# All 16 tiles of x loaded at once at the start of the projection, in place of two buffers in turn

## The reference

```
p = x @ w_in                       # (tokens, 2560) -> q | k | v | glu_a | glu_b
u = glu_a * sigmoid(glu_b)         # conv path: depthwise, width 31, LayerNorm, swish
o = differential attention(q, k, v)        # prompt: causal; sample: over the paged cache
x = LayerNorm(alpha * x + concat(o, conv) @ w_o)
x = LayerNorm(alpha * x + MoE(x))          # 64 experts, top 8, one shared expert
```

## Time and profile before

| what | us |
|---|---|
| median of 3 runs | 4477.3 |
| lowest, highest | 4462.62, 4480.28 |
| the profiled execution | 4473.9 |
| its span | 4472.2 |

### The profile page before, as it was taken

The page is one execution under the profiler, slowest core; times in us unless marked ns, Lnnn a source line. Parts: engine busy times, 40 slices in busy tenths (PEclk is TensorE's granted clock), DMA queues, the critical chain, the costliest instruction groups (busy, mean ns, idle before and its releaser), DMA issues. The chain is left out here.

```text
span 4472.2 us, 68787 instructions
## 1 busy us (share of the span) xinstructions
PE 3796.6 (85%) x20727; PEld 2500.4 (56%) x20729; DVE 2218.8 (50%) x4207; ACT 1589.5 (36%) x3240; POOL 1237.1 (28%) x1067
## 2 busy tenths in 40 slices
PE   6999995888698898858882879999999999999970
PEld 3444443666566665634441656667666676677640
DVE  1700994777565554435556224544444443434438
ACT  1011212666554444424341224443334433433420
POOL 0102211000033333300000754444444444444430
PEclk7999997999899999988885999999999999999985
DMA  3003327340199999931113329997888977877956
GB/s 104 16 19 135 140 92 150 68 87 20 56 386 396 386 403 386 386 135 62 61 61 105 103 82 270 272 266 180 228 229 217 269 185 163 227 177 187 263 130 213
DMA packets 358934, 817.65 MB, mean 183 GB/s; under 512 B 31720, under 2 KB 211304, under 8 KB 320358
## 3 DMA queue, kind: packets, MB, share of 16 engines
q0 software_dynamic: 125600, 512.88, 38.4%
q1 hardware_dynamic: 233166, 302.54, 21.1%
HBM read 659.59 MB, written 156.10 MB: 182 GB/s over the span
## 5 line engine op out<-in xcount | busy, mean ns | idle before, releaser
L1586 POOL DMA_INDIRECT y_s<-y_rows,scatter_now x322 | 539.7, 1676 | 417.6 <-DVE scatter_now L1755 244.5
L1645 PE MATMUL y_ps<-down_w,hiddenT 128*128 (+1 forms) x1416 | 640.3, 595 | 1.4 <-DVE y_rows L1756 1.4
L201 PE MATMUL p_bank<-xT,wcol 128*128 128x512 f32 (+1 forms) x1600 | 600.1, 535 | 5.0 <-DMA wcol<-in_w_in_dram 3.3
L1654 PE MATMUL gate_up_ps<-gu_high,x_highT 128*128 128x512 f32 x1416 | 573.5, 405 | 35.1 <-DVE x_lowT L1737 23.8
L1656 PE MATMUL gate_up_ps<-gu_high,x_lowT 128*128 128x512 f32 x1416 | 557.2, 393 | 0.0
L1655 PE MATMUL gate_up_ps<-gu_low,x_highT 128*128 128x512 f32 x1416 | 555.4, 392 | 0.0
L201 PEld LDWEIGHTS p_bank<-xT,wcol 128*128 128x128 f32 x1600 | 281.2, 193 | 306.5 <-issue 304.7
L1645 PEld LDWEIGHTS y_ps<-down_w,hiddenT 128*128 128x128 f32 x1416 | 255.7, 191 | 258.7 <-issue 258.2
L1743 DVE TENSOR_TENSOR gu_low<-gu_raw,gu_high 128x1024 fp32r<-128x1024 f32 x260 | 301.1, 1221 | 111.4 <-ACT gu_high L1693 106.8
L1578 POOL DMA_INDIRECT x_rows<-x_s,gather_now x179 | 179.8, 1005 | 591.5 <-DVE gather_now L1731 522.0
L1765 DVE TENSOR_TENSOR hidden<-silu_gate,gate_up_ps 128x256 f32<-128x256 f32 x177 | 74.2, 419 | 520.9 <-ACT silu_gate L1715 520.9
(11 more groups left out here) (264 smaller groups left out, 5485.7 us busy)
## 6 DMA issues: line engine op xcount, KB each, us to landing
gu_raw<-in_w_gate_dram SPq DMA_DIRECT2D x64, 1024.0 KB, 12.0
gu_raw<-in_w_up_dram SPq DMA_DIRECT2D x64, 1024.0 KB, 15.6
down_w<-in_w_down_dram SPq DMA_DIRECT2D x64, 1024.0 KB, 6.6
wcol<-in_w_in_dram SPq DMA_DIRECT2D x20, 512.0 KB, 3.9
x_s<-x SPq DMA_DIRECT2D x17, 512.0 KB, 2.6
xin<-in_x_prompt_dram SPq DMA_DIRECT2D x16, 512.0 KB, 3.6
out_dram<-rows POOLq DMA_DIRECT2D x8, 1024.0 KB, 7.7
k_high<-k_high_s POOLq DMA_DIRECT2D x16, 512.0 KB, 23.9
```

The lines of the kernel that those rows point to most:

```text
L201: mm = nc.tensor.matmul(bank[c][:, 0:n], wcol[u][:, k, :], xT[:, k, s:s + n], start=(k == 0), stop=(k == KT - 1))
L1586: pool.indirect_dma_start(out=g.y[half], out_offset=bass.IndirectOffsetOnAxis(ap=to[half][:], axis=0), in_=y[half][:], in_offset=None, com ...
L1645: mm = nc.tensor.matmul(y_ps[half][:], hT[:, k, :], down[:, w(half, k)], start=(k == 0), stop=(k == F // P - 1))
L1654: nc.tensor.matmul(out, x_high[:, k, :], both(gu_high, k), start=(k == 0), stop=False)
```

## The change

The 16 tiles of x get 16 places in SBUF: the two `xin` buffers, and for the other 14 halves of the prompt's part of the four units, of the gate, of `conv_sum` and of `rows1`, all of which the projection writes later. SyncE issues the 16 loads one behind the other with no wait. They count on four semaphores, one for tiles 0 and 1, one for 2 to 5, one for 6 to 10, one for 11 to 15; TensorE waits for the whole of a tile's group. The memset of `xin0` moves to behind VectorE's copy of tile 1; the sample's load is issued behind it, behind all 16, and counts on the first group's semaphore (48 in all). The loops over pairs on TensorE, ScalarE and VectorE become straight code over 17 tiles.

```diff
+        room = [xin[0][:], xin[1][:]] + [t[:, at + half * D:at + (half + 1) * D] for t, at in
+                                         [(glu, PAST) for glu in units] + [(gate, 0), (conv, 0)] for half in range(2)]
+        room += [rows[1][:].rearrange("p t f -> p (t f)")[:, half * D:(half + 1) * D] for half in range(2)]
...
-        x_in, w_arrived = (x_in0, x_in1), (w_in0, w_in1)
+        w_arrived = (w_in0, w_in1)
+        x_in = sems(nc, ctx, *[f"x_in{t}" for t in range(4)])
+        GROUP, PART = [0, 2, 6, 11, QT], [0] * 2 + [1] * 4 + [2] * 5 + [3] * 5
...
-            def load_x(i):
-                for u in range(2):
-
-                    wait(sp, xt_ready, (2 * i + u - 1) * 2)
-                    sp.dma_start(xin[u][:], g.x_prompt[ds(i * 2 * P + u * P, P), :]).then_inc(x_in[u], 16)
-            loop(sp, QT // 2, load_x)
+            for t in range(QT):
+                sp.dma_start(room[t], g.x_prompt[t * P:(t + 1) * P, :]).then_inc(x_in[PART[t]], 16)
             sp.wait_ge(x_zeroed, 1)
             sp.dma_start(xin[0][0:TAIL, :], g.x_sample).then_inc(x_in[0], 16)
 
-            sp.wait_ge(x_in[0], 16 * (QT // 2 + 1))
+            sp.wait_ge(x_in[0], 48)
             sp.dma_start(g.x_tail, xin[0][:]).then_inc(tail_out, 16)
...
-            def turn_x(u, tile, loaded):
-                pe.wait_ge(x_in[u], loaded)
+            def turn_x(u, tile):
+                n = PART[tile] if tile < QT else 0
+                pe.wait_ge(x_in[n], 16 * (GROUP[n + 1] - GROUP[n]) if tile < QT else 48)
+                x = room[tile if tile < QT else 0]
                 for half, copied in ((0, xt_act), (1, xt_dve)):
 
                     wait(pe, copied, tile - 1)
                     for k in range(4):
                         mm = nc.tensor.transpose(bank[2 * u + half][:, k * P:(k + 1) * P],
-                                                 xin[u][:, (4 * half + k) * P:(4 * half + k + 1) * P], g.ident[:])
+                                                 x[:, (4 * half + k) * P:(4 * half + k + 1) * P], g.ident[:])
                     mm.then_inc(xt_ready, 1)
-
-            def turn_pair(i):
-                for u in range(2):
-                    turn_x(u, 2 * i + u, 16 * i + 16)
-            loop(pe, QT // 2, turn_pair)
-            turn_x(0, QT, 16 * (QT // 2 + 1))
+            for tile in range(TT):
+                turn_x(tile % 2, tile)
...
-            loop(dve, QT // 2, keep_pair)
-
-            dve.wait_ge(xt_ready, 2 * (QT - 1))
-            nc.vector.memset(xin[0][:], 0.0).then_inc(x_zeroed, 1)
-            keep_x(0, QT, SEQ)
+            for tile in range(TT):
+                keep_x(tile % 2, tile, tile * P)
+                if tile == 1:
+                    nc.vector.memset(xin[0][:], 0.0).then_inc(x_zeroed, 1)
```

More of the change, by code:

```diff
@@ L119, in in_projection @@
         bank = [ctx.enter_context(nc.psum_tensor(f"p1_bank{b}", [P, 512], F32)) for b in range(8)]
-        (small_in, state_turned, state_kept, zeroed, x_in0, x_in1, x_zeroed, xt_ready, xt_act, xt_dve, w_in0, w_in1,
+        (small_in, state_turned, state_kept, zeroed, x_zeroed, xt_ready, xt_act, xt_dve, w_in0, w_in1,
          acc_ready, feat_ready, glu_ready, last_turned, last_kept, last_out, conv_step, conv_out, stored0,
          stored1, rows_ps, rows_ready, rows_out0, rows_out1, tail_out, high_ready, low_ready, parts_out) = sems(
-            nc, ctx, "small_in", "state_turned", "state_kept", "units_zeroed", "x_in0", "x_in1", "x_zeroed",
+            nc, ctx, "small_in", "state_turned", "state_kept", "units_zeroed", "x_zeroed",
             "xt_ready", "xt_act", "xt_dve", "w_in0", "w_in1", "acc_ready", "feat_ready", "glu_ready", "last_turned",
@@ L332, in keep_x @@
                                       bank[2 * u + 1][:].rearrange("p (k t) -> p k t", k=4)).then_inc(xt_dve, 1)
-            def keep_pair(i):
-                for u in range(2):
-                    keep_x(u, 2 * i + u, i * (2 * P) + u * P)
-            loop(dve, QT // 2, keep_pair)
-            dve.wait_ge(xt_ready, 2 * (QT - 1))
-            nc.vector.memset(xin[0][:], 0.0).then_inc(x_zeroed, 1)
-            keep_x(0, QT, SEQ)
+            for tile in range(TT):
+                keep_x(tile % 2, tile, tile * P)
+                if tile == 1:
+                    nc.vector.memset(xin[0][:], 0.0).then_inc(x_zeroed, 1)
             dve.wait_ge(zeroed, H + 1)
```

## The result

The changed kernel takes 4431.5 us (median of 5 runs, 4428.4 to 4433.1) against 4476.2 us before (5 runs, 4462.6 to 4480.3). The ratio is 0.9915, with a 95% interval of 0.9903 to 0.9928: 0.85% or 38 us less, between 32 and 43. (The medians themselves lie 44.7 us apart, since the five runs of before fall into two groups, two at 4463 and three from 4476 to 4480; the text goes by the ratio.) The forecast was 4445 us, a gain of 32.4 us, in a range of 4430 to 4458. Two later comparisons with the same kernel gave 0.9905 [0.9887, 0.9922] and 0.9926 [0.9905, 0.9946], with medians of 4435.8 and 4435.2 us against 4471.3 and 4468.6 before; by these ratios the gain is 42 and 33 us.

What follows compares the result with a forecast made beforehand. The first stage was bound by serial x loads before the first product, then solid TensorE work. Gains of 29.4 us (earlier product) and 3.0 (clock) took 4473.9 to 4441.5; with 3.4 for the median, 4445 us, range 4430 to 4458.

Steps and rivals of the forecast that it cites:

- The step that decides: First stage: the first product, at 76.64 us, ends a serial chain of x loads; the change starts it 29.4 us earlier.
- The stream: x loads issued at once: 393 GB/s, last byte at 36.9 us, groups complete at 25.1, 31.8 and 38.4 us.
- the 1.5 us from last byte to landing: x loads: time added after a group's last byte passes until the group counts as complete, 1.5 us.
- The turning: TensorE's transposes of x: 1.09 us a tile at high clock, 1.97 at low; last tile turned by 46.5 us.
- the clock to be low for three tiles after the second wait: Turning from tile 6, after the wait until 31.8 us: three tiles of 1.97 us, then two of 1.09.
- The weights' load: Before the first product: wcol is there at 44.4 us, covered by the turning (47.2 us) by 2.8 us.
- 47.2: Start of the first product in the changed kernel, in us; 76.6 before, so 29.4 us gained.
- The clock in the products: Start of the projection's products: full clock from the first matmul saves 3.0 us more, bounds 0 and 3.
- the loads stream: Against the rival that x loads don't stream (4477 us) or their groups interleave (4459 us); chance 0.07.
- the clock falls for some microseconds only: Against the rival of low clock all through the turning: first product at 55.4 us, 4456 us in all; chance 0.10.
- the experts' stage still has one instruction packet: Against the slower rival: straight code shifts the experts' loop, fetched anew each turn, 4577 us; chance 0.05.

Runs made afterwards that it cites:

- e4: Kernel of e3, but SyncE issues each x load only when the tile four before is turned, so four are under way; median 4449.7 us (one run).
- e1: Kernel before with its loops over pairs of tiles as straight code; buffers, waits and loads stay; ratio to before 0.9985, median 4465.7 us.
- e8: Kernel before with ten unread transposes put ahead of TensorE's wait for each x tile; ratio to before 0.9991, median 4466.0 us.
- e0: The changed kernel run a second time, unchanged; ratio to before 0.9905, median 4435.8 us.
- e10: The changed kernel run a third time, unchanged; ratio to before 0.9926, median 4435.2 us.
- e3: Changed kernel with eight groups of x tiles in place of four; median 4435.5 us (one run).
- e5: Kernel of e3 with the first two wcol loads issued ahead of the wait for the sample; ratio to before 0.9906, median 4425.0 us.
- e11: Kernel of e5 with biases and taps loaded behind x_tail, taps turned after the first block of products; ratio to before 0.9911, median 4428.8 us.
- e7: Kernel of e5 with the four small loads (state, taps, biases) through ScalarE's queue; ratio to before 0.9928, median 4435.1 us.

## Why the prediction was right, and where its steps were off

*The step that decides* (the first product is the end of a chain of loads that are issued one turn at a time): shown, by e4 between the two kernels, and by e1 and e8, which change the code and the clock and leave that chain, at 75.4 and 75.7 us.

*The stream.* 393 GB/s were forecast, 401 measured. The last byte at 36.9: the rate falls at 36. But the groups were complete later than I added for, by the bursts at 26.39, 32.80 and 40.33 (said: 25.1, 31.8, 38.4). The step that failed is the 1.5 us from last byte to landing; it was 4 us for the last group. From 36 to 41 us 0.38 MB moved (75 GB/s in the mean); if the sample's 0.26 MB, queued behind x, are among them, x was nearly all through at 36 us. That this grows was not in the rows that I had used.

*The turning.* I said 1.09 us for a tile at the high clock, which is the burst with the modelled end of its last matmul; but tiles in a row follow each other in 0.87 us (41.26 to 44.75 is four of them). I also took the clock to be low for three tiles after the second wait; tiles 6 to 10 took 6.0 us in all in this profile and 4.6 in e0 (32.87 to 37.46), not 8.1. The clock did fall around a wait of 2.7 us in this profile, to 0.74 as the mean of 30 to 35 us; the price was 1.5 us for five tiles (6.0 less 5 x 0.87 and the last one's end, 0.2). In e0 it stayed at 1.00 over the same stretch with the same wait (2.68 us) and fell behind the next one, of 3.64. This agrees in kind with the Trainium skill's warning of waits between bursts (TensorE: Matmul & The Clock Gate, Part 1). Which wait it strikes differs from profile to profile. These errors have the other sign than the stream's, and the last turn ended at 45.8, for 46.5 said (48.2 and 47.2 in e0 and e10).

*The weights' load.* I called wcol covered by 2.8 us. It was not: with the sample landing at 40.9 and not at 39.1, wcol was there at 46.8 and was what ended the wait in the first profile. Of that wait of 1.03 us the last copy would have taken 0.83, as in the other two profiles, so wcol cost 0.2 us. e3 shows it as the next limit, with 3.92 us, and e5 takes it away. So 47.2 was hit (46.8, 49.1, 48.0) by terms that were off by 1 to 3 us in both directions, and that they cancelled is luck.

*The clock in the products.* 3.0 us were said; the group is 4.8 us shorter, and 4.9 in e0 and e10. But the profile of before was a long one here as well: e1 and e8, whose products start cold too, have 597.6 and 598.4 us, and against them the changed kernel (595.2 to 595.3) gains 2.3 to 3.2.

*The rest.* The stage ended 33.7, 31.3 and 32.2 us earlier in the three profiles, for 32.4. The whole moved by 38, 42 and 33 us by the three ratios; the intervals of the first (32 to 43) and the third (24 to 42) hold the forecast gain, that of the second (35 to 51) doesn't. Later stages scatter by 15 us whatever the kernel, and the profiled execution of before, against which the sum was made, was a long one there. The time itself was hit less well than the gain: 4431.5 lies 13.5 us below the forecast and 1.5 above the low end of the range. The forecast subtracts from a median of 4477.3 us over three runs; the later comparisons put the kernel before at 4467.9 to 4471.3, so some 6 to 9 us of the 13.5 lie in that starting point. No rival came true: the loads stream, the clock falls for some microseconds only, and the experts' stage still has one instruction packet.

## What to carry to other kernels

A row of loads of 512 KB, each released by the use of the one before last, ran at 165 GB/s; issued at once, into room that is written only later, they ran at 401, and the change as a whole was worth 0.85% here, since TensorE had nothing else to do meanwhile. Then ask what the same queue issues behind them: the first weights stood behind a wait for the last small load, and moving them ahead of it gave 3.4 us more in the profile (e5 against e3), which whole times don't resolve. Small loads with few or tiny rows cost something in either order: ahead of the stream, they held it by about 2 us (e11 against e5, one profile each); beside it in another queue, they came 13 us late.

## What was not expected of the hardware

- An 8 MB stream ends slowly: from 38 to 40 us the mean share of the 16 DMA engines is 0.16 and 0.11 (0.11 and 0.10 in e10, 0.38 and 0.21 in e0), and the last tiles are there 4 us or more after the rate has begun to fall. It did so with and without taps and biases ahead of it.
- 512 biases of 4 bytes, last of four small loads in a queue of their own beside a full stream, were there at 32.3 us (e7), against 18.5 to 19.2 us ahead of the stream in one queue.
- With 16 loads of 512 KB queued, the issue of one on SyncE grows from 0.43 to 1.1 us.
- TensorE at its high clock all through the turning (e8) shortened the time for a tile with two buffers only from 2.86 to 2.70 us: loads to landing went from 3.6 to 4.1 us.
